# Two transformer blocks on one core: the order of ScalarE's copies, the first convolution tap and the low halves of weights in a seven-product down projection

## The reference

```python
def conv_ffn(h, w_up, conv_w, conv_b, w_down):     # h: 528 tokens x 1024, hidden 2816
    u = h @ w_up                                   # 528 x 5632
    T = u.shape[1]
    up = jnp.pad(u, ((0, 0), (CONV_WIDTH - 1, 0), (0, 0)))
    c = conv_b + sum(conv_w[j] * up[:, j:j + T] for j in range(CONV_WIDTH))   # 3 taps
    g, val = jnp.split(c, 2, axis=-1)
    return (jax.nn.silu(g) * val) @ w_down         # 2816 -> 1024
...
h = h + conv_ffn(rms_norm(h, ffn_norm[i]), ffn_w_up[i], ffn_conv_w[i], ffn_conv_b[i], ffn_w_down[i])
```

## Time and profile before

| | |
|---|---|
| three runs | 1839.92, 1841.88, 1843.88 us, median 1841.88 us |
| profiled execution | 1843.74 us; its span 1841.9 us |
| PE busy | 1731.1 us, 94% of the span |
| DVE busy | 1267.0 us, 69% |
| ACT busy | 680.1 us, 37% |
| POOL busy | 332.7 us, 18% |
| mean granted TensorE clock | 0.967 of full speed |

### The profile page before, as it was taken

How to read it: one execution, slowest core, us unless ns; L and a number is a source line. 1 busy time by engine, 2 the same in 40 slices (tenths; PEclk the granted TensorE clock), 3 DMA queues, 4 the chain that set the end, 5 groups by cost and what they waited for, 6 DMA issues and landing times. The chain is left out here.

```text
span 1841.9 us, 34246 instructions
## 1 busy us (share of the span) xinstructions
PE 1731.1 (94%) x14377; PEld 1556.7 (85%) x14377; DVE 1267.0 (69%) x2176; ACT 680.1 (37%) x1248; POOL 332.7 (18%) x261
## 2 busy tenths in 40 slices
PE   7999989978998889999999879999899999999997
PEld 3777769768996589999999879889767999999886
DVE  4337695447546867898897856598886687777434
ACT  3264442242114643343343242321376322222222
POOL 0001012000000000665574642334301000000000
PEclk8999979989999999999999989999999999999999
DMA  7421400022441013323223122335200222232332
GB/s 291 166 81 48 180 14 4 14 104 70 139 116 35 2 47 120 90 79 127 81 70 127 58 69 72 113 104 145 69 2 25 92 92 92 92 93 92 103 103 69
DMA packets 52569, 160.60 MB, mean 87 GB/s; under 512 B 8400, under 2 KB 11472, under 8 KB 52288
## 3 DMA queue, kind: packets, MB, share of 16 engines
q1 hardware_dynamic: 48544, 152.76, 25.9%
q10 hardware_dynamic: 3872, 5.65, 1.1%
HBM read 146.32 MB, written 2.10 MB: 81 GB/s over the span
## 5 line engine op out<-in xcount | busy, mean ns | idle before, releaser
L741 PE MATMUL banks<-hn_hi,w_hi 128*128 128x264 f32 (+1 forms) x1920 | 550.8, 287 | 18.6 <-DVE hn_lo L1681 11.7
L742 PE MATMUL banks<-hn_lo,w_hi 128*128 128x264 f32 (+1 forms) x1920 | 544.7, 284 | 0.0
L743 PE MATMUL banks<-hn_hi,w_lo 128*128 128x264 f32 (+1 forms) x1920 | 544.0, 283 | 0.0
L741 PEld LDWEIGHTS banks<-hn_hi,w_hi 128*128 128x128 f32 x1920 | 363.3, 189 | 30.3 <-issue 26.5
L742 PEld LDWEIGHTS banks<-hn_lo,w_hi 128*128 128x128 f32 x1920 | 364.5, 190 | 0.1
L743 PEld LDWEIGHTS banks<-hn_hi,w_lo 128*128 128x128 f32 x1920 | 362.4, 189 | 0.0
L1301 ACT ACTIVATE w_hi<-raw 128x1024 fp32r<-128x1024 f32 x137 | 145.2, 1060 | 531.6 <-PE banks L743 521.0
L1674 DVE TENSOR_TENSOR w_lo<-raw,w_hi 128x1024 fp32r<-128x1024 f32 x107 | 130.9, 1224 | 99.9 <-ACT w_hi L1301 99.9
L741 PE MATMUL banks<-hn_hi,more_hi 128*128 128x264 f32 x352 | 99.9, 284 | 0.0
L742 PE MATMUL banks<-hn_lo,more_hi 128*128 128x264 f32 x352 | 99.7, 283 | 0.0
L743 PE MATMUL banks<-hn_hi,more_lo 128*128 128x264 f32 x352 | 99.7, 283 | 0.0
(11 more groups left out here) (493 smaller groups left out, 4029.0 us busy)
## 6 DMA issues: line engine op xcount, KB each, us to landing
raw<-in_weights SPq DMA_DIRECT2D x207, 512.0 KB, 3.5
ring<-in_weights SPq DMA_DIRECT2D x50, 512.0 KB, 4.4
arena<-arena SPq DMA_DIRECT2D x80, 66.0 KB, 2.0
arena<-arena ACTq DMA_DIRECT2D x64, 66.0 KB, 2.4
arena<-in_gate_w SPq DMA_DIRECT2D x8, 512.0 KB, 3.5
h<-in_xT SPq DMA_DIRECT2D x2, 1024.0 KB, 6.6
arena<-in_alibi SPq DMA_DIRECT2D x1, 1024.0 KB, 7.7
out_t<-h SPq DMA_DIRECT2D x2, 512.0 KB, 2.9
```

Source lines behind the costliest of these rows:

```text
L741: mm(o, w[0][:, j, :], x[0][:, k, lo:hi], start=first, stop=False)
L742: mm(o, w[0][:, j, :], x[1][:, k, lo:hi], start=False, stop=False)
L743: ins_ = mm(o, w[1][:, j, :], x[0][:, k, lo:hi], start=False, stop=last)
```

## The change

Four things are changed.

1. **Low halves.** `POOL_LOWS` is empty for the first two stretches: DVE makes all seven low halves of a quarter there. POOL's sums for the next quarter now wait for DVE's low half of S3.
2. **First tap.** ACT does the first convolution tap and the bias (`conv_first`), after DVE's read of PSUM and ahead of the silu; DVE waits for `conv_first` and does two taps instead of three.
3. **Third stretch.** ACT's high half of plain product 21, and DVE's low half of it, move from ahead of the stretch into its first quarter, behind step j = 4 (on DVE behind the adds of the third copy). The norm of a quarter's two tiles moves from the quarter's end to the same place in the next quarter; the last one stays at the end.
4. A semaphore is freed elsewhere (`g_ostd` is counted on `g_osq`), with the same waits.

In the diff the functions up to the first `ffn0_norm_pair(3)` are ACT's (POOL's wait ahead of them apart), those behind it DVE's.

```diff
-    POOL_LOWS = ((S4_AT, S3_AT), (S4_AT, S3_AT), SUM_ORDER)
+    POOL_LOWS = ((), (), SUM_ORDER)
...
-                if S1_AT not in POOL_LOWS[e]:
-                    pool.wait_ge(S["w_split_d"], lows_d(e, r, S1_AT))
-                pool.wait_ge(S["w_split_p"], lows_p(e, r, S3_AT))
+                if S3_AT in POOL_LOWS[e]:
+                    pool.wait_ge(S["w_split_p"], lows_p(e, r, S3_AT))
+                else:
+                    pool.wait_ge(S["w_split_d"], lows_d(e, r, S3_AT))
...
+        def conv_first(g):
+
+            act.wait_ge(S["u_evac"], g + 1)
+            if g % 2 == 0 and g >= 4:
+                act.wait_ge(S["prod_done"], g // 2 - 1)
+            elif g % 4 == 1 and g > 4:
+                act.wait_ge(S["x_sum"], 4 * (g // 4 - 1) + 2)
+            elif g % 4 == 3 and g > 4:
+                act.wait_ge(S["p_lo_done"], 7 * (g // 4))
+            A(v_c[:, g % 4, :], v_in[:, g % 4, 2:T2 + 2], ACT.Identity, scale=col("conv_w", 2 * N_UP + g), bias=col("conv_b", g)).then_inc(S["conv_first"], 1)
...
                 after_down(c, q, j)
-            if c == 2:
-                for k in range(2 * q, 2 * q + 2):
-                    act.wait_ge(S["res_done"], 8 + k + 1)
-                    norm_tile(4, k, lambda k: col("dsa_norm", k))
+                if c == 2 and j == 4:
+                    if q:
+                        ffn0_norm_pair(q - 1)
+                    else:
+                        product_highs(FT - 1)
...
                 after_up(g)
                 if g == 0:
                     norm_root(3)
+                conv_first(g)
                 if g % 2:
...
-            product_highs(FT - 1)
             for q in range(4):
                 ffn0_down(2, q)
+            ffn0_norm_pair(3)
...
             add(1, 0, s4, ALU.subtract).then_inc(S["d_added"], 1)
+            if c == 2:
+                if q:
+                    ffn0_norm_pair(q - 1)
+                else:
+                    plain_rest(FT - 1)
             after_down(c, q, 5)
...
-            for k in range(2 * q, 2 * q + 2):
-                ve.wait_ge(S["res_done"], 8 + k + 1)
-                norm_tile(4, k, lambda k: col("dsa_norm", k))
...
-                ve.wait_ge(S["u_evac"], g + 1)
...
+                ve.wait_ge(S["conv_first"], g + 1)
...
-                st.link(V.tensor_scalar(c, u[:, 2:T2 + 2], w[2], col("conv_b", g), ALU.mult, ALU.add))
...
-            plain_rest(21)
             for q in range(4):
                 ffn0_down(2, q)
+            ffn0_norm_pair(3)
```

More of the change, by code:

```diff
@@ L411, in build @@
         s1_scores s1_soft s1_exp s1_prob s1_trans s1_pt s1_pv s1_out v1_trans v1_tok
-        g_absz g_ln g_cum g_diff tables_in g_exp g_lvl g_score g_taken g_zero g_tr g_trc g_qk g_sc g_sd g_ops g_ost g_osq g_osum g_ovar g_ostd g_oinv g_orow g_done
+        g_absz g_ln g_cum g_diff tables_in g_exp g_lvl g_score g_taken g_zero g_tr g_trc g_qk g_sc g_sd g_ops g_ost g_osq g_osum g_ovar g_oinv g_orow g_done
                    r_prod r_masked r_tokps r_toksb
@@ L416, in build @@
             rope_in rope_read rope_done v_ch v_tr v_tok a_sc a_max a_exp a_prob a_tr a_pt a_pv a_o
-            hd_sq hd_sum hd_var hd_std hd_tr hd_done res_done u_evac conv_done silu_done a_ready
+            hd_sq hd_sum hd_var hd_std hd_tr hd_done res_done u_evac conv_first conv_done silu_done a_ready
             f_step f_sum x_sum p_lo_done d_tap d_added
@@ L1416, in product_highs, with ffn0_norm_pair @@
                 pair_high(p, j, x_sum[:, i, :])
+        def conv_first(g):
[7 more added lines that the diff above has]
+            A(v_c[:, g % 4, :], v_in[:, g % 4, 2:T2 + 2], ACT.Identity, scale=col("conv_w", 2 * N_UP + g), bias=col("conv_b", g)).then_inc(S["conv_first"], 1)
+        def ffn0_norm_pair(q):
+            for k in range(2 * q, 2 * q + 2):
+                act.wait_ge(S["res_done"], 8 + k + 1)
+                norm_tile(4, k, lambda k: col("dsa_norm", k))
         def ffn0_down(c, q):
@@ L1973, in after_down, with plain_rest, ffn0_norm_pair @@
                 weight_low(S_DSA + j // 2)
+        def plain_rest(m):
+            ve.wait_ge(S["a_hi_done"], 70 + m - 19)
+            V.tensor_tensor(plain_tile(p_lo, m), v_c[:, (2 * m + 1) % 4, :], plain_tile(p_hi, m).bitcast(F32), ALU.subtract).then_inc(S["a_ready"], 1)
+        def ffn0_norm_pair(q):
+            for k in range(2 * q, 2 * q + 2):
+                ve.wait_ge(S["res_done"], 8 + k + 1)
+                norm_tile(4, k, lambda k: col("dsa_norm", k))
         def ffn0_down(c, q):
@@ L2989, in _ @@
             act.wait_ge(S["g_ovar"], j + 1)
-            A(g_cols[:, 8 * j:8 * j + 8], g_cols[:, 8 * j:8 * j + 8], ACT.Sqrt).then_inc(S["g_ostd"], 1)
+            A(g_cols[:, 8 * j:8 * j + 8], g_cols[:, 8 * j:8 * j + 8], ACT.Sqrt).then_inc(S["g_osq"], 1)
         def r_tokens(k):
@@ L3287, in _ @@
         for j in range(2):
-            ve.wait_ge(S["g_ostd"], j + 1)
+            ve.wait_ge(S["g_osq"], 2 + j + 1)
             V.reciprocal(g_cols[:, 8 * j:8 * j + 8], g_cols[:, 8 * j:8 * j + 8]).then_inc(S["g_oinv"], 1)
```

3 lines of the change are left out of this document (removed).

## The result

| | before | changed |
|---|---|---|
| median of four runs each | 1841.97 us | 1828.88 us |
| all runs | 1839.92 to 1843.88 | 1828.10 to 1832.45 |
| ratio, 95% interval | | 0.9933, 0.9916 to 0.9950 |
| profiled execution | 1843.74 us | 1829.59 us |

The changed kernel is 13.1 us faster.

A forecast was written before the change was run, and what follows sets the result against it. PE was taken to lose time only in the three down stretches, most in the third, waiting for ACT's copies. 14.2 us there plus 2.3 us in the first two made 16.5 us less: 1826 us, range 1816 to 1834 us.

The forecast's parts named there:

- The copies of quarters 1 to 3: Third stretch: ACT's first copy of x is free at once, so three waits, 10.3 us, go.
- The first copy: Third stretch, quarter 0: behind first tap and silu, PE waits 0.5 us instead of 6.7 us.
- The plain low half: Third stretch, quarter 0: DVE's seven instructions, slowed by POOL to 1.15 us each, make PE wait 6.4 us.
- rival (a): POOL does not hold DVE up in quarter 0 or lacks work: wait 1.3 us, 1821 us; chance 0.17.
- The clock: Third stretch, quarter 0: 1.4 us lost to lowered clock after the wait for the plain low half.
- Quarters 1 to 3: Third stretch: waits at product 3 and the plain step, 3.8 us in sum, bounds 0 and 9 us.
- The first two stretches: DVE makes all low halves, x is read earlier: 1.2 and 1.1 us less, bounds -4 and +8 us together.
- if the first two stretches change by over 3 us: One of two signs that would show the prediction wrong; the other was short DVE instructions in quarter 0.
- rival (c): Slower: low halves on DVE make its quarter outgrow PE's in the first two stretches; 1848 us, chance 0.04.
- The first tap: Up groups: moving it to ACT is priced 0, up to 0.73 us at each of 44 groups if cover went.
- What improves is the start: First two stretches: x read about 2 us earlier, stall before product 3 of quarter 1 too short to drop the clock.
- (b): New waits are long, in first stretches or at product 3 and plain step: gain 9 us, 1833 us; chance 0.13.

The follow-up runs named there:

- The kernel with the copies first: POOL held back and norm later, plus ACT's second and third copy ahead of the high halves of blocks 1 and 3, all stretches: 1826.13 us.
- the pair of executions above: Two executions of the changed kernel, same code, DVE and POOL compared in the third stretch: stretch 59.72 and 58.92 us.
- the kernel with x first and POOL held back: Changed kernel with DVE's add of x ahead of block 5's low half in the third stretch, POOL's low halves delayed in quarter 0: 1823.27 us.

## Why the prediction was right, and where its terms were off

1826 us were forecast, with 1822 to 1830 us for the likeliest case, and 1828.88 us were measured. The mechanism went as written; the sizes were off by 4.6 us of 16.5: 5.7 us too much in the third stretch and 1.1 too little in the first two. That the time came within 2.9 us of the forecast is in part luck. Of the 14.1 us between the profiled executions, 2.2 arose outside the stretches, where nothing was forecast. 11.9 us off the median before give 1830 us, at the very edge of the likeliest case.

**The copies of quarters 1 to 3** were free at once and their 10.3 us are gone. **The first copy** was late by 0.57 us (0.5 forecast).

**The plain low half** was late next. The wait was 7.17 us (6.4 forecast). DVE's product ended at 1046.91 us, 7.58 us into the stretch, against 7.1 forecast, and the seven instructions took 8.56 us, not "Seven instructions at 1.15 us" or 8.1 us; PE came 9.03 us into it, as forecast to 0.3. That POOL holds DVE up here, the step on which rival (a) turned, is shown by the kernel with POOL held back.

**The clock** was priced at 1.4 us. This row of the changed kernel shows what it was:

```profile
1051.20:1061.40 10.20, 5.87 (x26) 5.87 (x27) 5.87 (x7) 0.72 (x2) 4.81 (x5) 0.50 0.01 2
```

PE worked for 5.87 us of 10.20 at 1.2 GHz and would have needed half of that at 2.4, so 2.9 us were lost. It covers all 21 matmuls of the plain step and the first of quarter 1. The clock had fallen while PE stood still. That quarters 1 to 3 would run at full clock was wrong for the first 1.1 us of quarter 1.

**Quarters 1 to 3** were forecast with 0, 0.9 and 0.1 us at product 3 and 1.0, 1.5 and 0.3 us at the plain step. Measured were 0, 1.21 and 0, and 1.53, 2.05 and 0.59: 5.4 against 3.8 us. The places and their order were right. The quarters lasted 12.9, 14.4 and 11.5 us, not 11 to 12 each.

**Not counted** were the rest, 1.6 us: 59.72 less 42.1, 13.12 and 2.9. The stretch before, counted in the same way, has 0.4 us of it: 68.21 less 42.1, less 16.95 of waits and 8.7 for the half clock (the prediction put all of that remainder, 9.3 us, down to the clock). So 1.2 us are new. Gaps too short to be listed as waits grew by 0.4 us; the rest is not accounted for. Together: 0.1 + 0.8 + 1.5 + 1.6 + 1.6 = 5.6 us, and 14.2 less 5.6 is 8.6, where 8.49 were measured.

**The first two stretches** gave 1.45 and 1.98 us (1.2 and 1.1 forecast). As foreseen the wait before product 3 of quarter 1 fell, from 2.2 to 1.58 us in the first and 0.59 us in the second, the half clock behind it went, and later quarters gave a part back (in the first, 0.40 us in quarter 2 and 0.96 where it was 0.88 in quarter 3). In the first stretch the clock is nearly all of it: PE's waits come to 3.76 us in all, where they were 3.95. By the prediction's own list it would be wrong "if the first two stretches change by over 3 us"; together they changed by 3.4, so that sign, taken for the sum, came up. Its bounds for both were -4 and +8 us, and neither stretch by itself changed by more than 2. That DVE would outgrow PE, rival (c), didn't happen. Small waits of 0.24 to 0.28 us for copies were not foreseen. Those before product 6 come with the low halves: POOL's sum comes a little later, since it now waits for DVE, and ACT's high half of it stands in front of the third copy. The kernel with the copies first shows that they hide others. The one before product 2 of the first stretch comes with the first tap on ACT, ahead of silu and copy: it is in the kernel with the tap alone and not in the one with the low halves alone.

**The first tap** costs nothing in the up groups: 92.8 and 69.6 us with it and without it. What I had wrong is what it brings by itself. "What improves is the start" named the missing tap and POOL's missing low halves together, and the experiments show that in the first two stretches the tap does nothing without the other.

**The rivals.** The kernel with POOL held back is rival (a) put into effect, and it was priced too high: 1821 us, 5 less than the forecast, against 1825.47 us measured and 3.6 us off the stretch. The wait became 1.74 us (1.3 forecast), but no less of the stretch ran at half clock. Of (b), long new waits, a part came true: 7.17 and 5.4 us of wait and a lowered clock, a gain of 8.5 us in the third stretch where (b) had put 9 for the whole; the first two stretches made up the difference.

The Trainium skill (SBUF — State Buffer, section "SBUF: two separate sides") says of the shared port pair that whichever starts first holds it for a whole instruction and the other blocks. The traces agree, in the pair of executions above and in the 1.22 us of a DVE instruction beside POOL (0.42 to 0.70 us alone). When both have work queued, the runs show turns, one each, and not DVE first.

What stays open: I did not run a kernel in which only the clock differs, so how much of the later quarters' waits comes from the clock before them is not separated. Nor can I say when the clock will fall, and between some of these kernels it is the larger part of the difference.

## What to carry to other kernels

A wait that is moved away from an engine's queue comes back at the next item of the queue that is really full. Here that was VectorE's: new orders moved PE's wait between the plain low half, the add of x and product 3, and only what shortened the queue (POOL silent, POOL's work taken over) moved the stretch by more than 2.4 us. So before an order is changed, add up what stands on the engine between the late input and each thing that PE will ask for.

Work given to GpSimd is not free for VectorE when both read two operands from SBUF: count some 0.8 us here for each VectorE instruction that meets one (5.4 us over the seven). A low half costs VectorE 0.47 us of its own, less than what it loses when GpSimd makes it.

## What the runs showed of the hardware

**Turns between DVE and POOL.** With both queues full, DVE instructions with two SBUF operands and POOL instructions started in strict turn. Each of the seven on DVE took 1.06 to 1.49 us, where it takes 0.42 to 0.70 alone. POOL pays too: two low halves of 128x384 took 1.95 us with DVE idle and 2.57 to 2.63 us with DVE busy, 0.3 us more for each.

**Adds that read PSUM are exempt.** The add of an accumulator, `h<-h,banks`, takes 0.41 to 0.43 us each time in the changed kernel, also the 13 times that it lies wholly beside an instruction of POOL. `h<-h,taps` of the same size takes 1.24 us there. In the kernel with only the first tap, DVE and POOL at one time:

```profile
811.16 1.09 DVE L2007 TENSOR_TENSOR h<-h,banks 128x264 f32<-128x264 f32 x3
...
810.90 1.19 POOL L1249 TENSOR_TENSOR w_sum<-w_sum,raw 128x384 f32<-128x384 f32 x1
```

Three adds in 1.09 us, all but the end of the last beside one sum. So the same sum can cost DVE three times as much by way of a copy in SBUF.

**The clock after short waits.** It fell to half after PE had stood still for 2.2, 2.7 and 3.7 us, and within the waits of 6.7 and 7.2 us. With POOL held back it fell after 1.74 and 1.93 us, but in the kernel with x first and POOL held back not after 1.73 us at the same place, and in the changed kernel not after 2.05 us. The length of the one wait does not settle it in these traces.
